# Three reorderings in a fused attention and recurrence kernel: two gates, forty-eight transposes, one spread

## What is computed

```
o = softmax(q k^T + bias) v                    # first layer
y = (o * silu(gate)) @ w_out

flat = blocks of kc (and of vc) + pos_emb      # third layer, compression
k_cmp, v_cmp = silu(flat @ w1) @ w2
p_cmp = masked_softmax(q k_cmp^T)              # q not rotated
q_rot, k_rot = partial_rope(q), partial_rope(k)
o = g0 * p_cmp v_cmp + g1 * o_sel + g2 * o_win
o_nsa = o * silu(g_nsa)

state = state*w + (state @ -kk) (kk*a) + v k   # third layer, recurrence
y = state @ r                                  # per head
y = groupnorm(y) + bonus
out = x + concat(o_nsa, y * silu(g_rwkv)) @ w_out
```

## Time and profile before

| what | value |
|---|---|
| median of 3 runs | 1164.83 us (1164.63 to 1166.54) |
| the profiled execution, its own time | 1169.72 us |
| its span, first to last instruction | 1167.9 us |
| mean granted clock of TensorE | 0.986 of full speed |
| PE busy | 1101.9 us, 94% of the span |
| DVE, ACT, POOL busy | 692.1, 554.9, 463.6 us |
| chain that ended last | PE 79%, DVE 9%, POOL 4%, ACT 4% |

### The profile page before, as it was taken

The page is one execution under the profiler, slowest core; times in us unless marked ns, Lnnn a source line. Parts: engine busy times, 40 slices in busy tenths (PEclk is TensorE's granted clock), DMA queues, the critical chain, the costliest instruction groups (busy, mean ns, idle before and its releaser), DMA issues.

```text
span 1167.9 us, 26342 instructions
## 1 busy us (share of the span) xinstructions
PE 1101.9 (94%) x10855; PEld 940.8 (81%) x10855; DVE 692.1 (59%) x1436; ACT 554.9 (48%) x1141; POOL 463.6 (40%) x391
## 2 busy tenths in 40 slices
PE   3999999899999999999999999989899999999996
PEld 2999998789998998756699998967577788677763
DVE  5647777862327327888822437315885798535546
ACT  4335456873425342488834346432785352244431
POOL 4787765687334545501053334402003444112100
PEclk9999999899999999999999999999999999999999
DMA  8443334423222232300033123361101222400001
GB/s 223 142 109 109 109 109 138 107 68 99 73 73 73 73 109 77 104 1 1 2 109 101 56 65 134 100 198 37 37 2 37 72 73 101 118 4 22 3 3 72
DMA packets 74041, 91.79 MB, mean 79 GB/s; under 512 B 2202, under 2 KB 66851, under 8 KB 73795
## 3 DMA queue, kind: packets, MB, share of 16 engines
q1 hardware_dynamic: 70832, 80.22, 22.0%
q0 software_dynamic: 2416, 8.26, 2.9%
q10 hardware_dynamic: 674, 1.64, 0.5%
HBM read 85.85 MB, written 4.26 MB: 77 GB/s over the span
## 4 chain that ended last, share of the span: by engine, by line
PE 79%; DVE 9%; POOL 4%; ACT 4%; issue 2%; DMA 2%; ACTq 1%; DVEq 0%; POOLq 0%
PE banks L578 63%; PE banks L803 10%; PE banks L947 2%; ACT arena L1552 1%; POOL ring_parts L3061 1%; PE banks L1146 1%; DMA arena<-rpb_rows 1%; POOL arena L3132 1%; POOL arena L3125 1%; PE banks L670 1%; ACT arena L1988 1%; PE banks L1363 1%; DVE arena L2178 1%; DMA ring<-in_cmp_w_v 1%; DMA vrow<-in_final_norm_g 1%
## 5 line engine op out<-in xcount | busy, mean ns | idle before, releaser
L3061 POOL TENSOR_TENSOR ring_parts<-ring,ring_parts 128x512 fp32r<-128x512 f32 (+1 forms) x184 | 244.4, 1362 | 369.3 <-ACT ring_parts L1583 278.2
L578 PE MATMUL banks<-ring_parts,arena_parts 128*128 128x256 f32 x1856 | 322.1, 283 | 0.0
L578 PEld LDWEIGHTS banks<-ring_parts,arena_parts 128*128 128x128 f32 x1856 | 271.4, 190 | 2.2 <-DVE stat L2624 1.4
L578 PE MATMUL banks<-ring_parts,hT_parts 128*128 128x256 f32 x1024 | 221.8, 284 | 3.8 <-POOL ring_parts L3061 2.9
L1552 ACT ACTIVATE arena<-banks 128x512 f32<-128x512 f32 (+6 forms) x315 | 144.6, 525 | 120.0 <-PE banks L578 96.4
L578 PE MATMUL banks<-arena 64*64 64x64 f32 (+6 forms) x2544 | 174.5, 294 | 10.8 <-ACT arena L1552 3.6
L578 PEld LDWEIGHTS banks<-ring_parts,hT_parts 128*128 128x128 f32 x1024 | 171.1, 191 | 5.0 <-POOL ring_parts L3061 3.7
L578 PEld LDWEIGHTS banks<-arena 64*64 64x64 f32 (+2 forms) x2544 | 115.2, 143 | 59.3 <-issue 20.0
L578 PE MATMUL banks<-arena_parts,ring_parts 128*128 128x512 f32 x448 | 147.6, 401 | 2.8 <-POOL ring_parts L3061 2.8
L578 PE MATMUL banks<-hT_parts,ring_parts 128*128 128x512 f32 x320 | 114.4, 396 | 0.0
L1583 ACT ACTIVATE ring_parts<-ring 128x2048 fp32r<-128x2048 f32 (+1 forms) x47 | 88.4, 1881 | 40.8 <-PE banks L578 40.1
(11 more groups left out here) (313 smaller groups left out, 1763.4 us busy)
## 6 DMA issues: line engine op xcount, KB each, us to landing
ring<-in_a_w_in SPq DMA_DIRECT2D x16, 1024.0 KB, 5.5
ring<-in_w_in SPq DMA_DIRECT2D x15, 1024.0 KB, 5.5
ring<-in_b_w_in SPq DMA_DIRECT2D x10, 1024.0 KB, 5.1
ring<-in_ple_w_gate SPq DMA_DIRECT2D x8, 1024.0 KB, 5.0
arena<-rpb_rows POOLq DMA_DIRECT2D x16, 256.0 KB, 3.7
ring<-in_a_w_out SPq DMA_DIRECT2D x4, 1024.0 KB, 5.1
ring<-in_b_w_out SPq DMA_DIRECT2D x4, 1024.0 KB, 5.4
ring<-in_w_out SPq DMA_DIRECT2D x4, 1024.0 KB, 5.0
```

What stands on the lines that cost most here:

```text
L578: return nc.tensor.matmul(o, l, r, start=start, stop=stop)
L3061: nc.gpsimd.tensor_tensor(rounded(r), r, read_back(high_slot(n)[:, o:o + m // 4]), ALU.subtract)\
```

## The change

Four edits. In the first layer both `tanh_a` calls of the last weight block stand ahead of the loop over j on ScalarE, and both `gate_a` calls stand behind `frontA(1)` on VectorE. In the compression the transposes of a tile become a function `turned_c(i)`: tile 0 goes between the two halves of `hid` (with its wait for C_rope), tiles 1 and 2 follow `hid`, tile 3 follows `vcmp`; `scores_c(2)` moves ahead of `trans_c(0)`. ScalarE's program follows: tile 0, then the high part of Cog0, then the tanh of `hid`, tiles 1 and 2, `hidT`, tile 3. In the tail `spread_job(2)` moves from ahead of `solved(3)` into the middle of an output piece behind `state_step(3, 0)`, `finish(2)` and `gate(2)` on VectorE move behind `state(3, 0)`, and `state_step(3, 1)` with its `state(3, 1)` is left out; a wait for the state of the first chunk takes its place on TensorE.

```diff
@@ TensorE, compression @@
+            def turned_c(i):
+                for name, src in (("qp", q2), ("qr", q2r)):
+                    b = begin((name, i), "a")
+                    for j in range(4):
+                        ins = nc.tensor.transpose(b[:, j * P:(j + 1) * P], src[:, i, j * P:(j + 1) * P], ident)
+                    end(ins)
+                b = begin(("kz", i), "a")
+                for m in range(4):
+                    ins = nc.tensor.transpose(b[:, m * P:(m + 1) * P], kd[:, i, m // 2, (m % 2) * P:(m % 2) * P + P], ident)
+                end(ins)
...
                     used3(("W1K", 0))
                     used3(("W1V", 0))
+                    pe.wait_ge(S("C_rope"), 4)
+                    turned_c(0)
             end(ins, "hid")
             used3(("W1K", 1))
             used3(("W1V", 1))
-            pe.wait_ge(S("C_rope"), 4)
-            for i in range(NT):
...
+            turned_c(1)
+            turned_c(2)
             evacuated(pe, "hid")
             b = begin("hidT", "a")
...
+            turned_c(3)
             gate_c(1)
             evacuated(pe, ("kz", NT - 1))
             pe.wait_ge(S("C_cmp"), 12)
             scores_c(0)
             scores_c(1)
             gate_c(2)
+            scores_c(2)
             trans_c(0)
             trans_c(1)
-            scores_c(2)
             scores_c(3)
@@ TensorE, tail @@
             p = NT - 1
-            spread_job(p - 1)
             solved(p)
...
             state_step(p, 0)
             out_part(1, 0, 1, 2, hold=None)
-            state_step(p, 1)
+            spread_job(p - 1)
             out_part(1, 0, 1, 2, hold=None)
+            pe.wait_ge(S("R_state"), 2 * p + 2)
             state_outputs(p)
@@ ScalarE, first layer @@
+            tanh_a(len(SEVEN) - 1, 1)
+            tanh_a(len(SEVEN) - 1, 0)
             for j in range(8 + 2):
                 if j < 8:
                     expA(j)
-                if j < 2:
-                    tanh_a(len(SEVEN) - 1, 1 - j)
@@ ScalarE, compression @@
-            b = take(act, "hid")
-            nc.scalar.activation(thh, b[:, 0:256], ACT.Tanh, scale=0.5).then_inc(S("C_thh"), 1)
-            act.wait_ge(S("C_clear"), 3)
-            for i in range(NT):
-                if i == 2:
-                    high(HI[("Cog", 0)])
...
+            act.wait_ge(S("C_clear"), 3)
+            turned_c(0)
+            high(HI[("Cog", 0)])
+            b = take(act, "hid")
+            nc.scalar.activation(thh, b[:, 0:256], ACT.Tanh, scale=0.5).then_inc(S("C_thh"), 1)
+            turned_c(1)
+            turned_c(2)
             b = take(act, "hidT")
...
             give(ins, "hidT")
+            turned_c(3)
             high(HI[("Cog", 1)])
@@ VectorE, first layer @@
                 if j < 8:
                     frontA(j)
+                if j == 1:
+                    gate_a(len(SEVEN) - 1, 1)
+                    gate_a(len(SEVEN) - 1, 0)
...
-                if j < 2:
-                    gate_a(len(SEVEN) - 1, 1 - j)
@@ VectorE, tail @@
             p = NT - 1
-            finish(p - 1)
-            gate(p - 1)
             maps(p)
             add_half(1, 1, 0)
             state(p, 0)
-            state(p, 1)
+            finish(p - 1)
+            gate(p - 1)
             add_half(1, 0, 1)
```

## The result

The changed kernel takes 1159.49 us (median of four runs, 1158.61 to 1160.44), the kernel before 1165.68 us (four runs, 1164.63 to 1168.41). The ratio is 0.9941, with a 95% interval of 0.9921 to 0.996: faster by 6.2 us by the medians and 6.9 by the ratio, with 4.7 to 9.2 us in the interval. The forecast was 7.9 us and 1156.9 us, with 1154.3 to 1160.5 as range.

What follows compares the result with a forecast made beforehand. TensorE, busy 94% of the span, was taken as the bound. Gains of 0 (attention), 7.1 (compression) and 0.8 us (tail) sum to 7.9, taking the median 1164.83 to 1156.9 us, range 1154.3 to 1160.5.

Steps and rivals of the forecast that it cites:

- edit 2: Compression: reordered transposes, Cog0's high part and scores shorten TensorE's path by 7.1 us.
- Edit 1: First attention: two gates later gain 0 (range -2.6 to +0.7), covered by GpSimd's 9.57 us fetch and bias chain.
- the 1.6 us of `gate_c(0)`: Compression: gate_c(0) without the low clock takes 5.64 us instead of 7.23, a gain of 1.6 us.
- the 6.0: Compression: gate_c(0) starts at 781.9 instead of 787.90, a gain of 6.0 us.
- Edit 3: Tail: 0.65 us ahead of solved(3) plus 0.61 for state_step(3, 1), less 0.45 for transposes; 0.8, bounds 0.3 to 0.85.
- The step for the spread: Tail: dropping state_step(3, 1) gains 0.61 us, the spread's four transposes back on the path cost 0.45.
- The clock did not fall in the compression: Rival, chance 0.20: the clock falls again in the compression, losing 2.1 us, giving 1159.0 us.
- Cog0 landed: Rival, chance 0.08: in the compression Cog0's load lands 3.9 us late, giving 1160.8 us.
- The attention gained nothing: Rival, chance 0.12: the first attention gains too, up to VectorE's 2.57 us wait, giving 1154.3 us.
- The gates of Cog1: Rival of no change, chance 0.03: in the compression Cog1's gates wait for ScalarE, giving 1164.0 us.
- nothing made it slower: Rival, chance 0.02: the clock stays down from hid through the compressed scores, losing 14.6 us, giving 1171.5 us.
- The margin ahead of `mean_job(3)`: Tail: VectorE's moved finish(2) and gate(2) leave 0.6 us before mean_job(3); any excess reduces the 0.8 us gain.

Runs made afterwards that it cites:

- edit 3 alone: Only the tail's part of the change (spread moved, last state step left out) put into the kernel before: ratio 0.9987 (0.9971 to 1.0002).
- edits 1 and 3 alone: Two separate runs on the kernel before: only the first attention's last two gates later, ratio 1.0006; only the tail's part, ratio 0.9987.
- the kernel with the scores inside the gates: Changed kernel with compressed scores and first trans_c moved into gate_c(1) and gate_c(2), VectorE's gate operations into its exponential waits: ratio 0.9942 to the kernel before.
- the parts alone: The attention, compression and tail parts of the change, each put alone into the kernel before: ratios 1.0006, 0.9947 and 0.9987.
- ScalarE's order: Kernel before with one change on ScalarE: high part of Cog0 ahead of the tanh of hid; ratio 0.9981 (0.9968 to 0.9994), stage 47.92 us.
- TensorE's alone: Kernel before with one change on TensorE: tile 0's transposes between the two halves of hid; stage 52.90 us, no ratio given.

## Why the prediction came out as it did

**The time** of 1159.49 us is inside the range, 2.6 us above the forecast. The mechanism of each edit was right, and one term of edit 2 was mis-sized.

**Edit 1** at 0 fits the ratio, which allows 1.2 us of gain to 2.7 of loss, and its cover was right: GpSimd restarts at 211.7 to 212.6 in the six profiles with the edit and at 211.8 to 213.1 in the eight without it.

**Edit 2, the steps.** Taken 2.44 us earlier, the transposes of tile 0 were forecast at 770.46 and came at 770.41; the second half of `hid` from 771.76, and came at 771.87; the high part of Cog0 to 776.86 (776.65); the wait for the bank 1.1 us (0.67); `gate_c(0)` at 779.46 (779.17). `gate_c(0)` took 5.73 us where 5.64 were taken, `turned_c(3)` 1.28 for 1.3, and the moved scores gave 0.94 for 0.85. The second `trans_c` was named as a mark at 803.4 and came at 804.08; the mark was wrong by itself, since `scores_c(2)` now stands ahead of it. `scores_c(3)`, behind it in both orders, came some 7.3 us earlier (its first matmul at 811.64 before, at 801.91 + 2.44 after).

**Edit 2, the size.** The sum of 7.1 is the difference between this order and *one execution* of the old one, and as such it measured 7.4. The step that failed is the reading of the earlier trace rows as a rule: "after each hole the granted clock is 0.50 for 3.4 us", so that "the holes cost more than their length". From it came the 1.6 us of `gate_c(0)` and a part of the 6.0: `gate_c(0)` started 16.68 us into the stage before, 14.26 with edit 3 alone and 10.39 after, so 2.4 of the 6.3 us that it measured were the one execution's, 1.66 of them by the second half of `hid` (5.33 us against 3.67). The prediction had added that "the stretches of the sum have nothing of that difference that I can see", the 4.9 us between the profile and the median; they had. The same order without falls takes 49.64 us, so the work that the edit takes away is 49.64 - 46.20 = 3.4 us; the other 3.9 us are 3.2 of low clock and 0.8 of a later landing of W1V (a hole of 1.92 against 1.15), which an execution has or has not. Of the five profiles with the whole old order (before three times, edits 1 and 3 alone) four had both falls, none of those with edit 2 had one in the stage.

What a fall costs here can come back elsewhere: with the holes filled the stage had neither fall and the timed runs gained 0.5 us by the clock, and the kernel with the scores inside the gates had 20.1 us at 0.50 where the changed kernel had 13.7. For edit 2 some of it stayed: its timed gain of 6.2 us lies between the 3.4 and the 7.4, its interval (3.8 to 8.5 us) leaves the 3.4 out, and the clocks of the timed runs give it at most 2.7 (+- 1.5) us by the clock and 3.1 (+- 1.2) by the rest. That a sum made against one execution came so near is in part luck: nothing in its rows said how often the two falls come. That the clock would not fall in the changed compression came true, but the reason given for it, shorter holes, is not shown, since edit 3 alone had no fall behind a hole of 2.84 us.

**Edit 3** was forecast at 0.8 with an upper bound of 0.85, and gave 1.2 us alone. The 0.65 ahead of `solved(3)` measured 0.67. The step for the spread was taken as 0.61 - 0.45 = 0.16 and is 0.36 (from the end of `state_maps` to `state_outputs(3)`: 7.26 us before, 6.90 after and with edit 3 alone), so that was too low; the remaining 0.2 us stood in `state_maps`, which the edit doesn't touch. The margin ahead of `mean_job(3)` held.

**The rivals.** The clock did not fall in the compression in any of the six profiles that have edit 2's order on both engines. Cog0 landed 0.2 us ahead of the forecast. The attention gained nothing. The gates of Cog1 waited for nothing, and nothing made it slower. A rival was missing: that the gain of the clock comes back as low clock in other stages. With the filled holes it is what happened, as far as the estimate reaches; for edit 2 the estimate (2.7 +- 1.5 us against 3.2) cannot tell how much came back. Nor did 1.9 us bound the difference of two runs of before: the 26 beside the parts alone differ by 8.0 (1162.50 to 1170.49).

What stays open is what makes the clock fall at one place in one execution and not in the next. Where W1V's hole was 1.46 to 1.96 us (before three times, edit 1) both falls came, where it was 1.15 and 1.32 (edit 3, ScalarE's order) neither; these are six profiles, and a fall in `gate_c(3)` with the holes filled shows that such a list is not the whole of it. Open too is where the filled holes lose their 2.1 us.

## What to carry to other kernels

Price a hole by its length from one profile, and add nothing for the clock behind it until several executions show the fall at the same place and an edit has shown that the time follows. Compare the stage in profiles as the work, take the clock out of it by the busy time at the lower level, as an upper bound where a wait follows, and let the timed runs, their clocks included, say what is left. Judge two orders on two engines that hand work to each other as one edit: here ScalarE's order alone won 1.7 of edit 2's 3.4 us, TensorE's alone nothing.

## What the runs showed of the hardware

With one program, PE's busy time at clock 0.50 was 25.7, 30.7 and 29.1 us in three executions, with stretches at different places (385 in two of them, 496 in the third). With idle transposes in the two holes (12 in 1.53 us and 24 in 2.78 us) the one profile had no fall at their place and the kernel was no faster, 1.0014 (1.0002 to 1.0027): its PE time at 0.50 was 23.4 us, of which 10.2 in one stretch from 933.2 on.
